# The experts' down product: 96 rows of slots as one stationary operand, results stored as whole rows

## The reference, cut to what matters

```python
D_MODEL, N_EXPERTS, EXPERT_FF = 1024, 16, 512
h = silu(einsum('nd,edf->nef', t, w_g)) * einsum('nd,edf->nef', t, w_u)
h = h * gate[..., None]              # gate: (n, 16), two nonzero entries a token
out = einsum('nef,efd->nd', h, w_d)
```

## Time and profile before

| | |
|---|---|
| runs | 1917.14, 1914.15, 1914.95 us; median 1914.95 |
| profiled execution | 1916.52 us; span from first to last instruction 1914.9 us; mean granted clock 0.896 |
| TensorE busy (matmuls) | 1620.2 us, 85% of the span |
| TensorE weight loads | 1044.7 us, 55%, overlapping the matmuls |
| VectorE, ScalarE, GpSimd busy | 618.5, 396.7 and 117.8 us |
| moved by DMA | 410.01 MB, mean 214 GB/s |
| largest group: gate and up, line 1356 | 363.9 us busy |
| down product, line 1376 | 171.7 us busy |

### The profile page before, as it was taken

One profiled execution on the slowest core, in us unless ns is written; L12 is line 12 of the kernel. 1 busy time (PEld: TensorE's weight loads), 2 busy tenths in 40 slices (PEclk: granted clock), 3 DMA queues, 4 the chain that ended last, 5 costly groups with the idle time before them and its releaser, 6 DMA issues.

```text
span 1914.9 us, 36097 instructions
## 1 busy us (share of the span) xinstructions
PE 1620.2 (85%) x15137; PEld 1044.7 (55%) x15137; DVE 618.5 (32%) x1528; ACT 396.7 (21%) x973; POOL 117.8 (6%) x194
## 2 busy tenths in 40 slices
PE   4999887886879498989935999999989859989893
PEld 2435655564556455555522766667656545555552
DVE  3231354444430311111123566666651121111112
ACT  1011344443430110100102333333320011101010
POOL 0002012212120100000020000000000010000001
PEclk9999898888889699999966999999979959999996
DMA  9275256766581479999871444444422368999973
GB/s 304 88 271 173 75 185 210 233 201 212 181 304 57 166 258 373 371 388 359 334 231 34 109 127 127 127 127 127 153 76 67 123 221 307 380 369 370 387 270 92
DMA packets 228179, 410.01 MB, mean 214 GB/s; under 512 B 16664, under 2 KB 97273, under 8 KB 227961
## 3 DMA queue, kind: packets, MB, share of 16 engines
q1 hardware_dynamic: 187488, 326.39, 48.8%
q0 software_dynamic: 16000, 53.16, 8.7%
q10 hardware_dynamic: 24524, 28.07, 5.0%
HBM read 366.46 MB, written 41.12 MB: 213 GB/s over the span
## 4 chain that ended last, share of the span: by engine, by line
PE 69%; DVE 7%; issue 5%; DMA 4%; ACT 3%; POOL 1%; POOLq 1%; ACTq 0%; DVEq 0%
PE bank L1356 19%; PE bank L1850 12%; PE bank L1376 9%; PE bank L2219 4%; PE bank L1058 3%; PE bank L767 3%; PE bank L807 2%; PE bank L1893 2%; PE bank L1904 2%; PE bank L1342 1%; PE bank L775 1%; PE bank L242 1%; PE bank L1111 1%; PE bank L1920 1%; PE bank L480 1%
## 5 line engine op out<-in xcount | busy, mean ns | idle before, releaser
L1356 PE MATMUL bank<-ring,arena 128*32 128x256 f32 x6144 | 363.9, 392 | 40.4 <-issue 38.5
L1356 PEld LDWEIGHTS bank<-ring,arena 128*32 128x32 f32 x6144 | 209.5, 113 | 178.8 <-issue 68.7
L1850 PE MATMUL bank<-xnT,ring 128*128 128x320 f32 x768 | 230.7, 458 | 0.9 <-ACT catT L1793 0.9
L1850 PEld LDWEIGHTS bank<-xnT,ring 128*128 128x128 f32 x768 | 151.5, 202 | 66.5 <-issue 15.1
L1376 PE MATMUL bank<-ring,arena 128*32 128x256 f32 x3072 | 171.7, 379 | 1.4 <-issue 1.4
L1477 DVE TENSOR_TENSOR arena<-arena,bank 128x128 f32<-128x128 f32 x96 | 27.7, 288 | 398.8 <-ACT arena L1421 398.8
L1376 PEld LDWEIGHTS bank<-ring,arena 128*32 128x32 f32 x3072 | 100.9, 110 | 66.1 <-issue 1.7
L767 PE MATMUL bank<-ident,ring 128*128 128x128 f32 x512 | 86.9, 315 | 35.6 <-DVE ring L943 18.8
L1421 ACT ACTIVATE arena<-bank 128x128 f32<-128x128 f32 x96 | 26.6, 277 | 402.4 <-PE bank L1356 402.4
L286 PE MATMUL bank<-ring,xnT 128*128 128x512 f32 x224 | 99.4, 605 | 6.6 <-DVE xnT L251 6.6
L767 PEld LDWEIGHTS bank<-ident,ring 128*128 128x128 f32 x512 | 63.2, 158 | 56.4 <-DVE ring L943 23.7
(11 more groups left out here) (342 smaller groups left out, 1976.7 us busy)
## 6 DMA issues: line engine op xcount, KB each, us to landing
ring<-in_w_expert_down SPq DMA_DIRECT2D x32, 2048.0 KB, 10.9
ring<-in_w_expert_gate SPq DMA_DIRECT2D x32, 2048.0 KB, 14.0
ring<-in_w_expert_up SPq DMA_DIRECT2D x32, 2048.0 KB, 19.4
ring<-in_cache_k SPq DMA_DIRECT2D x128, 256.0 KB, 3.5
ring<-in_cache_v POOLq DMA_DIRECT2D x128, 256.0 KB, 3.8
ring<-in_w_in_even SPq DMA_DIRECT2D x9, 2048.0 KB, 12.9
ring<-in_w_in_odd SPq DMA_DIRECT2D x16, 1024.0 KB, 9.9
arena<-x_slots ACTq DMA_DIRECT2D x32, 384.0 KB, 7.2
```

The costliest lines, as they stand in the source:

```text
L1356: mm = pe.matmul(bank[2 + s][pair_rows(p), 0:256].rearrange("p (q n) -> p q n", q=2), x_in[par][:, k, 32 * s:32 * s + 32], w[:, :, k, P * ...
L1850: mm = pe.matmul(bank[c % 3][:, 0:NT], w[:, k, P * (c % 4):P * (c % 4) + P], xnT[:, k, 0:NT], start=(k == 0), stop=(k == KC - 1))
```

## The change

The down product takes all 96 slots at once. `hid_t` is laid out as four chunks of 128x96, and each chunk is the stationary operand of two products with 512 moving columns, one for bank 6 and one for bank 7. ScalarE copies bank 6 (the first 512 output columns) when the first half is done, VectorE bank 7 after the second half; VectorE's copy moves behind its product of the third pass. `y_rows` holds whole rows of 1024, and `store_y` writes an expert's 96 rows with one DMA, issued behind silu of the third pass. Semaphore counts follow.

```diff
-        hid_t = part(7424, ST, P)
-        y_rows = part(7808, 2, ST, 256)
-        y_pick = part(9400, 2, 3, D_MODEL)
+        hid_t = part(7424, FC, CAP)
+        y_rows = part(7808, 2, D_MODEL)
+        y_pick = part(9856, 2, 3, D_MODEL)
...
-            def down(e, par, s):
-                if s == 0:
-                    slot_loaded(pe, 3 * par + 2, slots_before(l, 3 * par + 2) + e // 2 + 1)
-                    pe.wait_ge(sem("hid_t_set"), E + e + 1)
-                n = ST * (E + e) + s
-                wait_pos(pe, ["y_taken_a", "y_taken_d"][n % 2], n // 2)
-                for f in range(FC):
-                    for c in range(4):
-                        mm = pe.matmul(bank[6 + n % 2][pair_rows(c), 0:256], hid_t[:, s, 32 * f:32 * f + 32],
-                                       slot_f[3 * par + 2][:, f, 256 * c:256 * c + 256], start=(f == 0), stop=(f == FC - 1))
-                        if f == FC - 1 and c >= (1 if s < 2 else 2):
-                            mm.then_inc(sem("down_done"), 1)
+            def down(e, par):
+                slot_loaded(pe, 3 * par + 2, slots_before(l, 3 * par + 2) + e // 2 + 1)
+                pe.wait_ge(sem("hid_t_set"), E + e + 1)
+                for half in range(2):
+                    wait_pos(pe, ["y_taken_a", "y_taken_d"][half], E + e)
+                    for f in range(FC):
+                        pe.matmul(bank[6 + half][0:CAP, :], hid_t[:, f, :], slot_f[3 * par + 2][:, f, 512 * half:512 * half + 512],
+                                  start=(f == 0), stop=(f == FC - 1)).then_inc(sem("down_done"), 1)
...
-            def take_y(e, s):
-                n = ST * (E + e) + s
-                act.wait_ge(sem("down_done"), DN * l + 8 * e + (3, 6, 8)[s])
-                if s < 2:
-                    wait_pos(act, f"y{e % 2}_stored", 64 * (8 * l + e // 2))
-                act.copy(y_rows[:, e % 2, s, :], bank[6][:, 0:256]).then_inc(sem("y_taken_a"), 1)
+            def take_y(e):
+                act.wait_ge(sem("down_done"), DN * l + 8 * e + 4)
+                wait_pos(act, f"y{e % 2}_stored", 16 * (8 * l + e // 2))
+                act.copy(y_rows[0:CAP, e % 2, 0:512], bank[6][0:CAP, :]).then_inc(sem("y_taken_a"), 1)
 
             def store_y(e):
-                n = ST * (E + e + 1)
-                act.wait_ge(sem("y_taken_a"), (n + 1) // 2)
-                act.wait_ge(sem("y_taken_d"), n // 2)
-                for c in range(4):
-                    act.dma_start(y_dram[CAP * e:CAP * e + CAP, 256 * c:256 * c + 256].rearrange("(s r) n -> r s n", s=ST),
-                                  y_rows[pair_rows(c), e % 2, :, :]).then_inc(sem(f"y{e % 2}_stored"), 16)
+                act.wait_ge(sem("y_taken_a"), E + e + 1)
+                act.wait_ge(sem("y_taken_d"), E + e + 1)
+                act.dma_start(y_dram[CAP * e:CAP * e + CAP, :], y_rows[0:CAP, e % 2, :]).then_inc(sem(f"y{e % 2}_stored"), 16)
...
                 if e:
-                    for s in range(ST):
-                        if (ST * (E + e - 1) + s) % 2 == 0:
-                            take_y(e - 1, s)
-                    store_y(e - 1)
+                    take_y(e - 1)
                 if e < N_EXPERTS:
                     silu(e, 2)
+                if e:
+                    store_y(e - 1)
...
             def take_hidden(e):
                 dve.wait_ge(sem("hid_turned"), HT * l + e + 1)
-                dve.tensor_copy(hid_t, bank[5][:, 0:ST * P].rearrange("p (s n) -> p s n", s=ST)).then_inc(sem("hid_t_set"), 1)
...
+                dve.tensor_copy(hid_t.rearrange("p f (s r) -> p s f r", s=ST), bank[5][:, 0:ST * P].rearrange("p (s f r) -> p s f r", s=ST, f=FC)).then_inc(sem("hid_t_set"), 1)
+
+            def take_y(e):
+                dve.wait_ge(sem("down_done"), DN * l + 8 * e + 8)
+                wait_pos(dve, f"y{e % 2}_stored", 16 * (8 * l + e // 2))
+                dve.tensor_copy(y_rows[0:CAP, e % 2, 512:1024], bank[7][0:CAP, :]).then_inc(sem("y_taken_d"), 1)
...
-                if e:
-                    for s in range(ST):
-                        if (ST * (E + e - 1) + s) % 2 == 1:
-                            take_y(e - 1, s)
                 if e < N_EXPERTS:
                     hidden(e, 2)
+                if e:
+                    take_y(e - 1)
...
             for par in range(2):
-                pool.wait_ge(sem(f"y{par}_stored"), 512 * (l + 1))
+                pool.wait_ge(sem(f"y{par}_stored"), 128 * (l + 1))
```

More of the change, by code:

```diff
@@ L1392, in few_pe @@
                 if e:
-                    for s in range(ST):
-                        down(e - 1, 1 - e % 2, s)
+                    down(e - 1, 1 - e % 2)
                 if e < N_EXPERTS:
@@ L1562, in moe_act @@
                     act.sem_inc(sem(f"x{par}_rows"), 128)
-                    act.sem_inc(sem(f"y{par}_stored"), 512)
+                    act.sem_inc(sem(f"y{par}_stored"), 128)
                 act.sem_inc(sem("x_in_a"), N_EXPERTS)
-                act.sem_inc(sem("y_taken_a"), ST * N_EXPERTS // 2)
+                act.sem_inc(sem("y_taken_a"), N_EXPERTS)
                 gate_rows_act(act, l)
@@ L1580, in moe_dve @@
                 dve.sem_inc(sem("hid_t_set"), N_EXPERTS)
-                dve.sem_inc(sem("y_taken_d"), ST * N_EXPERTS // 2)
+                dve.sem_inc(sem("y_taken_d"), N_EXPERTS)
         def expert_piece(sp, l, e, par, q):
```

## The result

The changed kernel takes 1942.2 us (median of four runs, 1939.3 to 1945.9) against 1916.1 of the kernel before: ratio 1.0137, 95% interval 1.0114 to 1.0159, so 1.1 to 1.6% slower. The forecast was 1927 with a range to 1938: the direction was right, the size about half of what came. The profiled execution has a span of 1939.3 us against 1914.9, 24.4 more.

The account below looks back on a forecast made before the run. The prediction took weight supply, about 19.0 us a turn against TensorE's 16.82, to bound the expert loop. With turns of 18.78, closing turns and last products gave about +12, from 1914.95 to 1927 us; range 1919 to 1938.

Parts of the forecast that it names:

- The multiplication: Down product: 16 instructions of 0.43 us plus two switches of 0.14, 7.14 us instead of 5.18; turn 18.78.
- if the weights never had to be waited for: Expert loops with all slack eaten: layer 0 changes by +4.7 us, layer 1 by +3.6, together +8.
- Copies, order, store: Larger copies, their new places and the one-DMA store: cost nothing, at the end within 1 us a layer.
- Clock: First passes behind seven longer waits take 5.03 to 5.35 us instead of 3.45, partly at 1.2 GHz; none slow afterwards.
- The sum: Both expert loops: turns begin about as now up to expert 12, then closing turns and last products add about +12 us.
- the closing turns: Turns from expert 12 to each layer's end, supply outrunning them: +5.2 us in layer 0, +2.8 in layer 1.
- (1): Expert loop: down weights are released later, so weights come later; 19.3 us a turn, +20, 1935; chance 0.16.
- (2): Down product: a 96-column instruction takes less than 0.43 us, say 0.32, and supply binds as now; 1915; chance 0.12.
- the time of 1914: Down product at 4.2 us, from the skill's about 131 ns per 512-column product and two passes per instruction.
- (3): Store in long rows disturbs the weights: supply goes from 19.0 to 19.6 us a turn, +25, 1940; chance 0.05.

Follow-up runs that it names:

- runs without supply: Kernel before and changed kernel, each loading only the first 128 rows of each weight matrix from expert 2 on: 1858.0 and 1923.7 us.
- the later load: Changed kernel with down weights loaded one expert later in SyncE's queue, behind gate and up: 1925.4 us; same order in the kernel before: 1906.4 us.
- the split store: Changed kernel with each expert's store split again into four DMAs of 96 pieces of 1 KB: 1939.9 us.

## Why the prediction was right in direction and wrong in size

*The multiplication*: right. 16 instructions of 0.43 us, a piece of 7.04 where 7.0 was summed (6.86 + 0.14), the pass behind it 3.59; a turn of 18.81 against 18.78; the last down product 7.09 against 7.13. The sum "if the weights never had to be waited for", +8, is what the runs without supply and with the later load show: +6 and +9.5.

*Copies, order, store*: right. Neither ScalarE nor VectorE holds up a pass, and the split store makes no difference.

*Clock*: right. No slow pass is left.

*The sum*: wrong, in one step: "the supply's 19.0 stays above 18.78, so up to expert 12 turns begin about when they do now". It took the 19.0 us from start to start for a rate of the engines that TensorE's work leaves alone. For the kernel before that was nearly so: with the down load moved back, 18.9 remain. For the changed kernel it was not. The trace before showed the other limit already: chains of 22.8 to 23.7 us from an issue of down weights to the landing of the next up weights. The issue hangs on TensorE's own place in the turn, 13.4 us before and 15.4 after. With 13.4 two turns could not be shorter than 36.7 us, below twice 19.0, so the rate bound; only where the clock had slowed the first pass was the issue later and the chain the limit then as well (721.26 to 736.61 are 15.4 us, and 23.4 more lead to 759.97). With 15.4 in every turn it is 38.9, above twice 18.81, and the chain binds every pair up to expert 13: 19.45 a turn were measured. Ten turns grew by 4.3 us in each layer, where the forecast had next to nothing, and the two turns before them by 1.4 and 2.2, because the first wait, too, ends such a chain. That is the 12 us by which the forecast of +12 misses the measured 24.4; the closing turns came out within half a us of the sum in each layer, the last products at +1.64 for +1.68.

*Rivals*: (1) was this mechanism, with 19.3 a turn and 1935 as price and a chance of 0.16. The sign that the prediction gave for it, a turn of 19.3 or more, came with 19.45. What spoke against it, that some of the 23.3 us was queue, fits the kernel before, but not the one after, where the load in front runs out within 2 us of the issue. Its price lacked the opening turns and some 0.15 us a turn. (2) fell with the 0.43 us, and so did the time of 1914 by the rule of the Trainium skill that stood beside it ("TensorE: Matmul & The Clock Gate", Back-to-back issue gap). (3) fell with the split store and with the later load, which kept the store as it was.

## What to carry to other kernels

When a stage waits for loads, don't take the distance of its turns for the rate of the queue: write down from which instruction each load is released and how long it is from there to the wait that it ends, and add the two. A slower instruction ahead of a release costs its time again in that loop, even where the engine has slack; and a load that is needed late should not stand in the queue in front of one that is needed soon. Here the order of three loads was worth 17 us in the new kernel and 10 in the old one by the medians, 10.7 and 9.0 inside the loops of the traces.

## What the hardware showed beside this

A 96-column stationary operand streams 512 columns in 0.43 us, as the 128-column one did. A down piece costs about 0.2 us beside its 16 x 0.43 whether 32-column groups (7.04) or 128-column transposes and a wait of 0.09 (7.08) stand in front of it. Ninety-six pieces of 4 KB and 384 of 1 KB are the same to a queue that also carries the weights: 1942.2 and 1939.9 us, within the intervals. Waits of 4 to 7 us before a pass lengthened it from 3.45 to between 4.9 and 6.5 us, at a granted clock of 0.74 in one of 4.90 and 0.55 in the longest.
